# Middle four tiles of expert V rows: a spread activation matrix in DRAM and one pass over the V table

## Chip, core and metric

One core of a Trainium2 chip runs the whole program. The metric is the device time of one execution in microseconds. The profile names the engines PE (TensorE), DVE (VectorE), ACT (ScalarE), POOL (GpSimd) and SP (SyncE, which only issues transfers here); sixteen DMA engines move the data for all of them.

## Reference

One layer over 1024 tokens of width 1024, all in f32. First come two token mixers (a gated delta rule over four heads and a forgetting attention over eight), merged by two gates and put through a LayerNorm. Then comes PEER, the part that the change touches: each token picks 16 experts in each of 8 heads, 128 in all, out of 16384. Cut from the reference:

```python
def block(args):
    h_blk, e_blk, g_blk = args                     # 128 tokens, their 128 experts each, their gates
    u = jnp.take(u_tab, e_blk, axis=0)             # rows of 1024 floats
    act = jax.nn.gelu(jnp.einsum('td,tkd->tk', h_blk, u), approximate=False) * g_blk
    vv = jnp.take(v_tab, e_blk, axis=0)
    return jnp.einsum('tk,tkd->td', act, vv)
```

The result is added to 2**0.25 times the residual and put through a second LayerNorm. The U and the V table are 64 MB each (16384 rows of 4 KB).

## The kernel before

The tokens are cut into 8 tiles of 128 and 4 blocks (b = 0 to 3) of two tiles. `order()` writes out a list of 582 units (a step of the delta rule, an attention piece, a top-16 search and so on) that every engine walks in the same order; block b's mixers come first, then its choice of experts (`top`, `cand`, `sel`), which ends with the unit `idx`, where the chosen indices are transposed into `idxT`. The projections of block b + 1 are interleaved with the choice of block b; the last choice has none beside it.

The expert work runs alongside. After each unit every engine calls `experts(s)`, and the lists `DOTS` and `TOKS` that `pace()` plans say how much of it belongs to step s:

- A **U gather** (`gather_u`) is one indirect DMA from GpSimd: for one of the 128 choices of a tile, the 128 rows that its tokens chose, 128 x 4 KB, one row to a partition. VectorE multiplies it with the tile in `h_cur` and sums (one instruction, into a column of `dots`). When the 128 columns of a tile are there, ScalarE takes the gelu into `wgt`, VectorE multiplies with the gates, PE transposes, and ScalarE copies back into `dots`.
- A **V gather** (`gather_v`) is one indirect DMA too: the 128 rows that one token chose. Four such gathers make a quad. ScalarE spreads the weights into `wide32` (`spread`), and PE multiplies: for each of four tokens and two halves of 512 columns, one product with 32 columns of weights, which lands in the two PSUM banks `BY`. After the 32 quads of a tile VectorE adds the residual, takes the moments and normalises, and ScalarE stores the tile.

All gathers share `ring`, 18 places of 512 KB; from the place `WIDE` on, behind the last merge, 9 places in `arena` join it. `place_free` holds GpSimd until the reader of a place is done. At most `NU` = 16 U gathers and `NQ` = 8 quads are in flight. As planned by `pace()`, 768 U and 768 V gathers are done when the last `idx` ends; 256 of either kind remain for the tail. By stretches between the ends of `idx` (first half of block 0, second half, blocks 1, 2, 3, tail) the U counts are 106, 54, 188, 251, 169, 256 and the V counts 0, 64, 148, 248, 308, 256.

Of the kernel before, what the change touches and what calls it, by code (L numbers as in the profile page):

```python
# [10 lines left out]
D = 1024  # L11
# [20 lines left out]
NR = 18  # L32
NX = 9
NU, NQ = 16, 8
# [86 lines left out]

def pace():
# [3 lines left out]
    alone = UNITS.index(("top", NB - 1, 0))  # L126
    total = sum(share(kind, b) for kind, b, i in UNITS[first + 1:alone])
# [3 lines left out]
    dots, toks = [0], [0]  # L131
    ready, run, lately = 0, 0.0, 0
    for n, (kind, b, i) in enumerate(UNITS):
# [8 lines left out]
        else:  # L142

            run += share(kind, b) if n < alone else 0.0
# [5 lines left out]
    while dots[-1] < P * NT:  # L150
        dots.append(min(P * NT, dots[-1] + 4))
    dots += [P * NT] * 56
    opened = next(s for s in range(len(dots)) if dots[s] >= P) + 1
    for s in range(1, len(dots)):
        edge = P * (toks[-1] // P + 1)
        ready = dots[s] - P - LAG if dots[s] < P * NT else toks[-1] + 4
        step = 4
        if alone < s <= last + 1:

            begin = toks[alone]  # L160
            ready, step = begin + round((T * (NB - 1) - begin) * (s - alone) / (last + 1 - alone)), 8
# [7 lines left out]
    assert toks[-1] == P * NT and toks[-5] == P * NT  # L169
# [3 lines left out]
    for n in range(NT):  # L173
        for f in range(2, 32 // PHASE):
            assert phase_step(toks, n, f) < next(s for s in range(len(toks)) if toks[s] > P * n + 4 * PHASE * f)
    fetch = []
# [4 lines left out]
    for n in range(NT):  # L181
        assert begun[n] > dotted[n] and (n == 0 or begun[n] > summed[n - 1])
        assert n < 3 or fetch[n] >= summed[n - 3] + 2
        assert fetch[n] <= next(s for s in range(len(dots)) if dots[s] > P * n)

    place, upos, vpos = 0, [], []
    for s in range(1, len(dots)):
        du, dv = dots[s] - dots[s - 1], toks[s] - toks[s - 1]
# [8 lines left out]
    return dots, toks, dotted, begun, summed, fetch, upos, vpos  # L197

DOTS, TOKS, DOTTED, BEGUN, SUMMED, FETCH, UPOS, VPOS = pace()  # L200
# [4 lines left out]
def slots():  # L205

    begin = UNITS.index(("top", NB - 1, 0)) + 1
    at = UPOS + VPOS
    wide = min([UPOS[k] for k in range(DOTS[begin], P * NT)] + [VPOS[k] for k in range(TOKS[begin], P * NT)])
# [28 lines left out]
PLACED = UNITS.index(("idx", NB - 1, 0)) + 1  # L238
# [18 lines left out]
def item_loads():  # L257
# [8 lines left out]
    return value  # L266

LOADS = item_loads()
# [12 lines left out]
def transposed(n):  # L282

    return n // TT + 2 if n >= TT else n + 1

def build(nc, x, xT, w_qkv, w_z, w_sm, w_fqk, w_fv, w_mix, w_out, w_pq, conv_w, bias96, alog96,
          norm_w, ln, eu, ev, out):
    ctx = ExitStack()
    with ctx:  # L290
# [18 lines left out]
        d_h1 = dram("d_h1", SEQ, D)  # L309

# [15 lines left out]
        iota16 = sb("iota16", [P, TOPK])  # L326
# [7 lines left out]
        ring = sb("ring", [P, NR, D])  # L334
# [178 lines left out]
        s_yv, s_ys, s_y, s_out, s_h = sem("s_yv"), sem("s_ys"), sem("s_y"), sems("s_out", 3), sems("s_hc", 3)  # L513

# [5 lines left out]
        def place(p):  # L520

            if SLOT[p] < NR:
                return ring[:, SLOT[p], :]
            return arena[:, D * (SLOT[p] - NR + 1):D * (SLOT[p] - NR + 2)]

        hp = [banks[:, 1024 * (1 + k):1024 * (2 + k)] for k in range(2)]
        assert D * (NX + 1) <= after_rows and 32 % (2 * PHASE) == 0
# [13 lines left out]
        def _(sp):  # L541
# [210 lines left out]
        def _(pool):  # L752
# [7 lines left out]
            pool.iota(iota16[:, :], [[1, TOPK]], base=0, channel_multiplier=0, allow_small_or_imprecise_dtypes=True)  # L760
# [49 lines left out]
            def gather_v(k):  # L810
                n, i = divmod(k, P)
# [11 lines left out]
            for s in range(1, len(DOTS)):  # L823
                us, vs = range(DOTS[s - 1], DOTS[s]), range(TOKS[s - 1], TOKS[s])
# [1166 lines left out]
```

## Time and profile before

| | |
|---|---|
| Median of 3 runs | 3569.27 us (3568.06 to 3578.89) |
| Span of the profiled execution | 3575.8 us |
| Time of the profiled execution | not listed apart from its span; the span lies inside the range of the runs, 6.5 us above their median |
| Gathers (queue q0) | 1073.87 of 1290.18 MB moved |

The span runs from the first to the last instruction of the profiled execution.
### The profile page before, as it was taken

To read this page: it belongs to the slowest core of one execution; us is meant where nothing else is said; L and a number is where in the kernel's file an instruction comes from. 1 tells how busy PE (TensorE), PEld (TensorE's weight loads), DVE (VectorE), ACT (ScalarE), POOL (GpSimd) and SP (SyncE) were. 2 spreads that over 40 slices of the span, in tenths; PEclk is the share of its full clock that TensorE was granted. 3 is DMA by queue.
4 is the path that set the end of the run, shared out by engine and by line. 5 is a ranking of instruction groups with operands and counts; after the bars stand their busy time and mean duration, and the time that the engine had idled before them with its cause. 6 is when DMAs were issued, how large, how long until landed. Compare 5 with 4: busy or idle time off the path is not lost.

```text
span 3575.8 us, 37418 instructions
## 1 busy us (share of the span) xinstructions
PE 2446.3 (68%) x12224; PEld 1513.4 (42%) x12224; DVE 2097.0 (59%) x4939; ACT 655.0 (18%) x1652; POOL 2209.1 (62%) x2093
## 2 busy tenths in 40 slices
PE   8889993677976876667977877766797730133354
PEld 6676872444754544434735544433564310000000
DVE  5134899875477675554358776554447669744400
ACT  3331322332022213321003212321101000000000
POOL 1000577677547765677556766677767667777774
PEclk9899996888998987777988988867898865566588
DMA  5323999899989999999999999999999999999998
GB/s 171 91 87 136 363 401 360 336 392 402 409 312 373 400 412 360 350 381 384 415 402 351 408 405 394 369 377 371 398 413 410 409 410 409 410 409 409 409 410 324
DMA packets 367626, 1290.18 MB, mean 361 GB/s; under 512 B 39596, under 2 KB 68148, under 8 KB 362308
## 3 DMA queue, kind: packets, MB, share of 16 engines
q0 software_dynamic: 294912, 1073.87, 76.8%
q1 hardware_dynamic: 66760, 201.33, 15.2%
q10 hardware_dynamic: 5760, 12.59, 0.9%
q8 instruction: 98, 1.61, 0.2%
q14 instruction: 96, 0.79, 0.1%
HBM read 1274.65 MB, written 12.98 MB: 360 GB/s over the span
## 4 chain that ended last, share of the span: by engine, by line
PE 24%; DMA 22%; POOL 17%; DVE 16%; issue 15%; ACT 3%; DVEq 3%; ACTq 0%; POOLq 0%; SPq 0%
DMA ring<-in_ev,idxT 12%; PE banks L1570 10%; POOL ring L818 8%; DVE ring L1260 8%; POOL ring L804 8%; DMA ring<-in_eu,eidx 5%; PE banks L1580 4%; PE banks L1559 4%; DMA arena<-in_eu,eidx 3%; PE banks L1855 2%; PE banks L1702 1%; PE banks L1621 1%; DMA wslot<-in_w_mix 1%; POOL arena L818 1%; POOL arena L804 1%
## 5 line engine op out<-in xcount | busy, mean ns | idle before, releaser
L804 POOL DMA_INDIRECT ring<-in_eu,eidx x938 | 1044.4, 1113 | 875.5 <-DVE eidx L1529 393.4
L818 POOL DMA_INDIRECT ring<-in_ev,idxT x894 | 950.9, 1064 | 380.0 <-issue 245.7
L1559 PE MATMUL banks<-ring,wide 128*32 128x512 f32 x3576 | 631.5, 790 | 530.5 <-DMA ring<-in_ev,idxT 460.5
L1260 DVE CUSTOM_DVE_ANT_0 ring<-ring,h_cur 128x1024 f32<-128x1024 f32 x663 | 782.6, 1221 | 192.1 <-DMA ring<-in_eu,eidx 190.1
L1570 PE MATMUL banks<-arena,wslot 128*128 128x256 f32 (+2 forms) x3280 | 747.2, 386 | 21.9 <-DMA wslot<-in_w_pq 12.5
L1570 PEld LDWEIGHTS banks<-arena,wslot 128*128 128x128 f32 (+1 forms) x3280 | 622.4, 194 | 179.2 <-issue 70.9
L1559 PEld LDWEIGHTS banks<-ring,wide 128*32 128x32 f32 x3576 | 120.1, 130 | 851.7 <-DMA ring<-in_ev,idxT 431.5
L1260 DVE CUSTOM_DVE_ANT_0 ring<-ring,banks 128x1024 f32<-128x1024 f32 x275 | 329.3, 1217 | 110.8 <-DMA ring<-in_eu,eidx 106.8
L1580 PE MATMUL banks<-arena 128*128 128x128 f32 x1408 | 216.2, 312 | 42.3 <-ACT arena L995 26.1
L1580 PEld LDWEIGHTS banks<-arena 128*128 128x128 f32 x1408 | 202.9, 223 | 79.7 <-ACT arena L995 33.5
L1559 PE MATMUL banks<-arena,wide 128*32 128x512 f32 x520 | 138.6, 868 | 118.6 <-DMA ring<-in_ev,idxT 64.5
L1409 DVE TENSOR_REDUCE few<-banks 128x1 f32<-128x128 f32 (+3 forms) x64 | 48.4, 756 | 225.4 <-PE banks L1775 225.4
L1570 PE MATMUL banks<-ring,wslot 128*128 128x256 f32 (+1 forms) x656 | 151.4, 388 | 11.8 <-DMA wslot<-in_w_sm 7.4
L818 POOL DMA_INDIRECT arena<-in_ev,idxT x130 | 123.4, 949 | 40.3 <-issue 32.6
L1260 DVE CUSTOM_DVE_ANT_0 arena<-arena,banks 128x1024 f32<-128x1024 f32 x86 | 104.4, 1220 | 57.2 <-DMA arena<-in_eu,eidx 55.5
L1570 PEld LDWEIGHTS banks<-ring,wslot 128*128 128x128 f32 (+1 forms) x656 | 125.0, 193 | 30.1 <-issue 12.3
L1442 DVE TENSOR_TENSOR arena<-arena,banks 128x256 f32<-128x256 f32 x48 | 18.1, 418 | 195.2 <-PE banks L1570 195.2
L1550 PE MATMUL banks<-ident,wgt 128*128 128x128 f32 x8 | 2.7, 343 | 179.1 <-DVE wgt L1244 168.2
L1237 DVE SCALAR_TENSOR_TENSOR h_cur<-h_cur,banks 128x512 f32<-128x512 f32 x16 | 10.2, 680 | 188.6 <-PE banks L1559 188.6
L1559 PEld LDWEIGHTS banks<-arena,wide 128*32 128x32 f32 x520 | 24.4, 139 | 191.5 <-issue 78.2
L1575 PE MATMUL banks<-ident,arena 128*128 128x128 f32 x216 | 43.3, 348 | 83.2 <-DVE arena L1375 33.3
L1855 PE MATMUL banks<-wslot,arena 128*128 128x512 f32 x224 | 98.1, 595 | 2.9 <-issue 2.9
(302 smaller groups left out, 2810.9 us busy)
## 6 DMA issues: line engine op xcount, KB each, us to landing
wslot<-in_w_pq SPq DMA_DIRECT2D x64, 576.0 KB, 8.3
wslot<-in_w_mix SPq DMA_DIRECT2D x24, 1536.0 KB, 9.8
wslot<-in_w_qkv SPq DMA_DIRECT2D x48, 512.0 KB, 7.0
wslot<-in_w_fqk SPq DMA_DIRECT2D x32, 512.0 KB, 7.6
ring<-in_eu,eidx POOLq DMA_INDIRECT x938, 12.6
wslot<-in_w_out SPq DMA_DIRECT2D x7, 2048.0 KB, 10.4
ring<-in_ev,idxT POOLq DMA_INDIRECT x894, 12.4
wslot<-in_w_z SPq DMA_DIRECT2D x16, 512.0 KB, 6.7
```

Source lines behind the costliest of these rows:

```text
L804: pool.indirect_dma_start(out=place(UPOS[k]), out_offset=None, in_=eu, in_offset=bass.IndirectOffsetOnAxis(ap=eidx[:, n % (2 * TT), c // T ...
L818: pool.indirect_dma_start(out=place(VPOS[k]), out_offset=None, in_=ev, in_offset=bass.IndirectOffsetOnAxis(ap=idxT[:, n % (2 * TT), t:t + ...
L1260: dve.tensor_tensor_reduce(out=row, in0=row, in1=hp[0] if held else h_cur[:, n % 3, :] if n < NT - TT else hp[n % 2], scale=1.0, scalar=0. ...
L1409: dve.tensor_reduce(nm[:, r:r + 1], SB[b][r][:, 0:w], AX.X, ALU.max, negate=True).then_inc(s_sc[r], 1)
L1442: dve.tensor_tensor(mt[:, k, :], gates[:, k, :], B[3 * j + 1 - k][:, 0:T], ALU.mult)
L1559: last = pe.matmul(BY[k][32 * j:32 * j + 32, :], wide32[:, at:at + 32], place(VPOS[4 * q + j])[:, k * 512:(k + 1) * 512], start=(m == 0), ...
L1570: last = pe.matmul(bank, w[:, k0 + k, :], rhs[:, k, :], start=(k == 0), stop=(k == nk - 1))
L1575: last = pe.transpose(bank[:, h * P:(h + 1) * P], src[:, h, :], ident[:, :])
L1580: last = pe.matmul(bank[:, h * P:(h + 1) * P], lhs[:, h, :], rhs[:, h, :], start=start and (stop or h == 0), stop=stop and (start or h == ...
L1621: last = pe.matmul(PN[b][tt][:, :], xTs[b][:, k, tt * P:(tt + 1) * P], w[:, kk, :], start=(k == 0), stop=(k == KB - 1))
L1702: pe.matmul(B[4][:, :], ident[:, :], ident[:, None, :].to_broadcast([P, GH, P]), start=True, stop=False)
L1855: last = pe.matmul(WO[b][nh][tt][:, :], mixT[:, k, tt * P:(tt + 1) * P], w[:, k, :], start=(k == 0), stop=(k == KB - 1))
```

## The change

For tiles 2 to 5 (`DENSE`, tokens 256 to 767) no V row is gathered. Instead:

- **Spread.** For each of these tokens VectorE writes two 128x128 matrices, one comparing a row of 0 to 127 with the low 7 bits of each chosen expert, one comparing it with the high 7 bits and multiplied by the activation (`spots`). PE multiplies the two (one 128x128 product a token), which puts each activation at the place of its expert in a 128x128 grid, and ScalarE copies four such grids at a time from PSUM into `staged`. Each 16 tokens make 1 MB, which goes to the matrix `d_act` in DRAM (32 stores).
- **Product.** When all 512 tokens are spread and the last choice is done, SP reads the V table once, 128 pieces of 128 rows, into the eight slots of `wslot`, and `d_act` back in 16 pieces of 2 MB (runs of 512 bytes) into two places in `arena`. For each of the 128 pieces PE makes 8 products of 128 weight columns with 512 tokens, accumulated in the eight PSUM banks over all 128 pieces. ScalarE copies the eight banks out, PE transposes them, and VectorE and ScalarE finish tiles 2 to 5.
- **Order.** Tiles 6 and 7 keep their V gathers, which now begin behind the product, since that fills all banks. Their U gathers run beside it.
- **Room.** The ring has 13 places (five go to `staged` and to half of the comparison matrices), 12 U gathers and 5 quads may be in flight; seven places join at `WIDE`, which now lies at the start of the product. Tiles 6 and 7 take their dots from `h_cur` instead of a copy in PSUM.

As planned by the changed `pace()`, the U counts by the same stretches are 106, 54, 171, 229, 208, 256, the V gathers 0, 64, 128, 64, 0, 256, and the tokens spread 0, 0, 0, 184, 200, 128. Behind the last `idx` come the 128 remaining tokens with 80 U gathers; then `DENSE_AT`, and 176 U gathers beside the product.

```diff
-NR = 18
-NX = 9
-NU, NQ = 16, 8
+PLACES = 18
+NR = 13
+NX = 7
+DENSE = range(2, 6)
+ONE_BY_ONE = [n for n in range(NT) if n not in DENSE]
+HOT = range(P * DENSE[0], P * (DENSE[-1] + 1))
+STAGED = 16
+CHUNK = 8
+NCHUNK = P // CHUNK
+NV = 8
+NU, NQ = 12, 5
...
+        if HOT[0] <= toks[-1] <= HOT[-1]:
+            ready, step = edge - P + (dots[s] - edge) * P // (P - 24), 8
...
+        if toks[-1] > HOT[-1]:
+            if built is None:
+                built = s
+            step = 4
+            if dense[-1] < P or dense[max(0, s - 6)] < P:
+                ready = toks[-1]
+        dense.append(min(P, dense[-1] + 2) if built and s > built + 2 else 0)
         toks.append(max(toks[-1], min(ready // 4 * 4, edge, toks[-1] + step)))
...
+        d_act = dram("d_act", len(HOT) // STAGED, P, P * STAGED + 64)
...
+        staged = [ring[:, NR + 2 * k:NR + 2 * k + 2, :].rearrange("p a b -> p (a b)") for k in range(2)]
+        ones_at = [v.rearrange("p (t k c) -> p t k c", t=4, k=2) for v in (wide32[:, 0:D], ring[:, NR + 4, :])]
+        chunk = [arena[:, D + 4 * D * k:D + 4 * D * (k + 1)].rearrange("p (g c) -> p g c", g=len(HOT) // STAGED) for k in range(2)]
+        vtab = [wslot[:, k // 4, D * (k % 4):D * (k % 4 + 1)] for k in range(NV)]
+        yT = arena[:, D:5 * D].rearrange("p (k t) -> p k t", k=KB)
+        hy = arena[:, 9 * D:13 * D].rearrange("p (n c) -> p n c", n=len(DENSE))
+        SUM = [BY, B[0:2], B[2:4], B[4:6]]
...
+            sp.wait_ge(s_ixT, transposed(NT - 1))
+            for i in range(P):
+                c = i // CHUNK
+                if i % CHUNK == 0:
+                    if c == 0:
+                        for k in range(2):
+                            sp.wait_ge(s_stored[k], 16 * (len(HOT) // STAGED // 2))
+                    if c >= 2:
+                        sp.wait_ge(s_spot, len(HOT) // 4 + CHUNK * (c - 1))
+                    sp.dma_start(chunk[c % 2], d_act[:, :, c * CHUNK * STAGED:(c + 1) * CHUNK * STAGED].rearrange("g j x -> j g x")
+                                 ).then_inc(s_chunk[c % 2], 16)
+                if i >= NV:
+                    sp.wait_ge(s_spot, len(HOT) // 4 + i - NV + 1)
+                sp.dma_start(vtab[i % NV], ev[i * P:(i + 1) * P, :]).then_inc(s_w[i % NV // 4][i % 4], 16)
...
                 if p == WIDE:
-                    pool.wait_ge(s_hTe, TT * NB)
-                    pool.wait_ge(s_h1st, 16 * NB)
+                    for k in range(2):
+                        pool.wait_ge(s_stored[k], 16 * (len(HOT) // STAGED // 2))
+                    pool.wait_ge(s_spot, len(HOT) // 4)
+                    pool.wait_ge(s_ixT, transposed(NT - 1))
...
+                for k in range(hot(TOKS[s - 2]) // STAGED, hot(TOKS[s - 1]) // STAGED):
+                    act.wait_ge(s_sev, STAGED // 4 * (k + 1))
+                    act.dma_start(d_act[k, :, 0:P * STAGED], staged[k % 2]).then_inc(s_stored[k % 2], 16)
+                for q in range(hot(TOKS[s - 1]) // 4, hot(TOKS[s]) // 4):
+                    k, m = divmod(q, STAGED // 4)
+                    act.wait_ge(s_spot, q + 1)
+                    if m == 0 and k >= 2:
+                        act.wait_ge(s_stored[k % 2], 16 * (k // 2))
+                    act.activation(staged[k % 2].rearrange("p (i t) -> p t i", t=STAGED)[:, 4 * m:4 * m + 4, :],
+                                   BY[q % 2][:, :].rearrange("p (t i) -> p t i", t=4), ACT.Copy).then_inc(s_sev, 1)
+                if s == SUMMED[DENSE[0]]:
+                    act.wait_ge(s_spot, len(HOT) // 4 + P)
+                    for k in range(KB):
+                        act.activation(yT[:, k, :], B[k][:, :], ACT.Copy).then_inc(s_sev, 1)
...
+            def spots(q):
+
+                n, m = DENSE[q // 32], q % 32
+                cols, rows_ = expert_rows(n)
+                if m == 0:
+                    dve.wait_ge(s_ixT, transposed(n))
+                    dve.wait_ge(s_wm, n + 1)
+                    dve.drain()
+                    dve.tensor_scalar(rows_.bitcast(U32), cols, 7, None, ALU.logical_shift_right)
+                    dve.tensor_scalar(cols, cols, P - 1, None, ALU.bitwise_and)
+                    dve.drain()
+                    dve.tensor_copy(rows_, rows_.bitcast(U32))
+                    dve.tensor_copy(cols.bitcast(F32), cols)
+                    dve.drain()
+                    dve.wait_ge(s_w32, columns(n) + 1)
+                if q >= 2:
+                    dve.wait_ge(s_spot, q - 1)
+                if q == 0:
+                    dve.wait_ge(s_vq, T // 4)
+                for r in range(4):
+                    t = 4 * m + r
+                    dve.tensor_scalar(ones_at[q % 2][:, r, 0, :], iota[:, :], cols.bitcast(F32)[:, t:t + 1], None, ALU.is_equal)
+                    last = dve.tensor_scalar(ones_at[q % 2][:, r, 1, :], iota[:, :], rows_[:, t:t + 1], dots[:, n % 2, t:t + 1],
+                                             ALU.is_equal, ALU.mult)
+                last.then_inc(s_hot, 1)
...
                         pe.wait_ge(s_wm, n + 1)
-                        pe.wait_ge(s_yev, n)
+                        if n <= DENSE[0]:
+                            pe.wait_ge(s_yev, n)
+                        elif n in DENSE:
+                            pe.wait_ge(s_sev, 32 * (n - DENSE[0]))
+                        else:
+                            pe.wait_ge(s_yev, DENSE[0] + 1 if n - 1 in DENSE else n)
                         pe.transpose(BY[0][:, 0:P], wgt[:, :], ident[:, :]).then_inc(s_wT, 1)
...
+                    pe.wait_ge(s_hot, q + 1)
+                    if q >= 2:
+                        pe.wait_ge(s_sev, q - 1)
+                    for r in range(4):
+                        last = pe.matmul(BY[q % 2][:, r * P:(r + 1) * P], ones_at[q % 2][:, r, 0, :], ones_at[q % 2][:, r, 1, :],
+                                         start=True, stop=True)
+                    last.then_inc(s_spot, 1)
+                for i in range(DONE[s - 1], DONE[s]):
+                    c, ii = divmod(i, CHUNK)
+                    if i == 0:
+                        pe.wait_ge(s_sev, len(HOT) // 4)
+                        pe.wait_ge(s_ixT, transposed(NT - 1))
+                    if ii == 0:
+                        pe.wait_ge(s_chunk[c % 2], 16 * (c // 2 + 1))
+                    pe.wait_ge(s_w[i % NV // 4][i % 4], 16 * (LAST_LOAD.get((i % NV // 4, i % 4), 0) + i // NV + 1))
+                    acts = chunk[c % 2][:, :, STAGED * ii:STAGED * (ii + 1)]
+                    for k in range(KB):
+                        last = pe.matmul(B[k][:, :], vtab[i % NV][:, k * P:(k + 1) * P], acts, start=(i == 0), stop=(i == P - 1))
+                    last.then_inc(s_spot, 1)
+                if s == SUMMED[DENSE[0]]:
+                    pe.wait_ge(s_sev, len(HOT) // 4 + KB)
+                    for k in range(len(DENSE)):
+                        for half in range(2):
+                            last = transpose4(SUM[k][half], yT[:, 4 * half:4 * half + 4, k * P:(k + 1) * P])
+                        last.then_inc(s_spot, 1)
+                for q in range(alone(TOKS[s - 1]) // 4, alone(TOKS[s]) // 4):
```

## Rows read from the trace of the kernel before

**Rows 1.** The page: span, busy time of PE, gather queue, bytes

```profile
span 3575.8 us, 37418 instructions
...
PE 2446.3 (68%) x12224; PEld 1513.4 (42%) x12224; DVE 2097.0 (59%) x4939; ACT 655.0 (18%) x1652; POOL 2209.1 (62%) x2093
...
q0 software_dynamic: 294912, 1073.87, 76.8%
...
HBM read 1274.65 MB, written 12.98 MB: 360 GB/s over the span
```

**Rows 2.** Tile idxT: ScalarE's copies of the transposed choices, first and last start

```profile
L1174 ACT ACTIVATE idxT<-banks x3: 384/384/385, 1349.7 to 2900.8; 128x256 uint32<-128x256 f32 x3
L1169 ACT ACTIVATE idxT<-banks x2: 277/278/278, 573.9 to 765.6; 128x128 uint32<-128x128 f32 x2
```

**Rows 3.** Timeline of ScalarE, window 2126:2200: the copy behind block 2's choice

```profile
2172.23 0.38 ACT L1174 ACTIVATE idxT<-banks 128x256 uint32<-128x256 f32 x1
```

**Rows 4.** Windows between those choices: busy of five engines, PE clock, DMA share, GB/s

```profile
574.00:766.00 192.00, 115.68 (x706) 74.83 (x710) 172.54 (x488) 60.89 (x150) 134.00 (x124) 0.78 0.93 348
766.00:1350.00 584.00, 458.47 (x2121) 297.17 (x2113) 382.73 (x984) 112.00 (x298) 380.45 (x332) 0.88 0.99 385
1350.00:2172.00 822.00, 628.45 (x3126) 395.35 (x3126) 495.72 (x1175) 174.99 (x437) 560.91 (x503) 0.85 1.00 385
2172.00:2901.00 729.00, 547.09 (x2934) 312.25 (x2932) 396.14 (x994) 134.30 (x320) 514.34 (x483) 0.85 1.01 393
2901.00:3576.00 675.00, 200.93 (x1042) 37.11 (x1042) 328.78 (x541) 11.29 (x31) 465.68 (x496) 0.65 1.00 398
```

**Rows 5.** PE's waits in windows 766:1350, 1350:2172, 2172:2901: total us, times, longest

```profile
PE banks L1559 <- DMA ring<-in_ev,idxT: 85.5, 20, 13.1
...
PE banks L1559 <- DMA ring<-in_ev,idxT: 127.6, 34, 10.5
...
PE banks L1559 <- DMA ring<-in_ev,idxT: 113.8, 35, 7.2
```

**Rows 6.** Window 2705:2901, between the last merge and the last choice, columns as Rows 4

```profile
2705.00:2901.00 196.00, 145.97 (x855) 72.94 (x851) 121.37 (x524) 20.00 (x69) 139.81 (x144) 0.87 1.03 409
```

**Rows 7.** The page's costliest group on DVE: the U dots

```profile
L1260 DVE CUSTOM_DVE_ANT_0 ring<-ring,h_cur 128x1024 f32<-128x1024 f32 x663 | 782.6, 1221 | 192.1 <-DMA ring<-in_eu,eidx 190.1
```

**Rows 8.** The page's DMA issues: U gathers, median us to landing

```profile
ring<-in_eu,eidx POOLq DMA_INDIRECT x938, 12.6
```

**Rows 9.** Timeline of VectorE, window 1360:1368: four 128x128 TENSOR_SCALAR

```profile
1359.69 0.98 DVE L1347 TENSOR_SCALAR arena<-arena 128x128 f32<-128x128 f32 x4
```

**Rows 10.** Lines of PE by form: 128x128 products, and transposes

```profile
L1580 PE MATMUL banks<-arena 128*128 128x128 f32 x1408 | 216.2, 312 | 42.3 <-ACT arena L995 26.1 <-DVE arena L1388 9.4 <-ACT arena L992 4.1
...
L1575 PE MATMUL banks<-ident,arena 128*128 128x128 f32 x216 | 43.3, 348 | 83.2 <-DVE arena L1375 33.3 <-DVE arena L1355 22.1 <-DVE arena L1402 12.3
```

**Rows 11.** Lines of ScalarE by form: a PSUM bank of 128x512 copied

```profile
L1114 ACT ACTIVATE arena<-banks 128x512 f32<-128x512 f32 x31 | 18.5, 597 | 282.3 <-PE banks L1570 282.3
```

**Rows 12.** Timeline of PE, window 2660:2700: 128- and 32-column weights

```profile
2665.61 1.92 PE L1559 MATMUL banks<-ring,wide 128*32 128x512 f32 x16 [0.54 <-DMA ring<-in_ev,idxT]
2667.47 14.00 PE L1855 MATMUL banks<-wslot,arena 128*128 128x512 f32 x32
...
2690.49 3.64 PE L1559 MATMUL banks<-ring,wide 128*32 128x512 f32 x16 [6.14 <-DMA ring<-in_ev,idxT]
```

**Rows 13.** A window of unbroken PE work, columns as Rows 4

```profile
2590.00:2645.00 55.00, 55.00 (x280) 43.31 (x273) 22.82 (x44) 3.58 (x10) 34.08 (x31) 1.00 1.02 416
```

**Rows 14.** DMA issues: 2 MB load, 1 MB store, 512-byte pieces

```profile
wslot<-in_w_out SPq DMA_DIRECT2D x7, 2048.0 KB, 10.4
...
d_h<-arena SPq DMA_DIRECT2D x4, 1024.0 KB, 10.2
...
arena<-d_fv SPq DMA_DIRECT2D x4, 512.0 KB, 18.3
```

**Rows 15.** The chain that ended last, its last long piece

```profile
3537.50 26.86 DMA ring<-in_ev,idxT
```

More of the change, by code:

```diff
@@ L125, in pace @@
     last = UNITS.index(("idx", NB - 1, 0))
-    alone = UNITS.index(("top", NB - 1, 0))
-    total = sum(share(kind, b) for kind, b, i in UNITS[first + 1:alone])
+    total = sum(share(kind, b) for kind, b, i in UNITS[first + 1:last])
     second = UNITS.index(("att", 1, 0))
     levels = sum(share(kind, b) for kind, b, i in UNITS[first + 1:second])
-    dots, toks = [0], [0]
+    dots, toks, dense = [0], [0], [0]
     ready, run, lately = 0, 0.0, 0
@@ L142, in pace @@
         else:
-            run += share(kind, b) if n < alone else 0.0
+            run += share(kind, b) if n < last else 0.0
             if n < second:
@@ L149, in pace @@
         dots.append(max(dots[-1], min(want, ready, dots[-1] + 8)))
-    while dots[-1] < P * NT:
-        dots.append(min(P * NT, dots[-1] + 4))
-    dots += [P * NT] * 56
     opened = next(s for s in range(len(dots)) if dots[s] >= P) + 1
-    for s in range(1, len(dots)):
-        edge = P * (toks[-1] // P + 1)
[L156 to L161, printed above, removed]
+    built = None
+    s = 0
+    while len(dots) < len(UNITS) + 2 or toks[-1] < P * NT:
+        s += 1
+        if s == len(dots):
+            dots.append(min(P * NT, dots[-1] + 4))
+        edge = P * (toks[-1] // P + 1)
+        ready, step = dots[s] - P - LAG, 4
+        if HOT[0] <= toks[-1] <= HOT[-1]:
+            ready, step = edge - P + (dots[s] - edge) * P // (P - 24), 8
+        if s > last + 1:
+            ready, step = toks[-1] + 8, 8
         if s <= second:
@@ L167, in pace @@
             ready = toks[-1]
+        if toks[-1] > HOT[-1]:
[5 more added lines that the diff above has]
+        dense.append(min(P, dense[-1] + 2) if built and s > built + 2 else 0)
         toks.append(max(toks[-1], min(ready // 4 * 4, edge, toks[-1] + step)))
-    assert toks[-1] == P * NT and toks[-5] == P * NT
+    for _ in range(6):
+        dots.append(dots[-1])
+        toks.append(toks[-1])
+        dense.append(dense[-1])
     dotted = [next(s for s in range(len(dots)) if dots[s] >= P * (n + 1)) for n in range(NT)]
@@ L172, in pace @@
     summed = [next(s for s in range(len(toks)) if toks[s] >= P * (n + 1)) for n in range(NT)]
-    for n in range(NT):
+    for n in ONE_BY_ONE:
         for f in range(2, 32 // PHASE):
             assert phase_step(toks, n, f) < next(s for s in range(len(toks)) if toks[s] > P * n + 4 * PHASE * f)
+    for n in range(NT):
+        assert begun[n] > dotted[n] and (n == 0 or begun[n] > summed[n - 1])
+    for n in DENSE:
+        assert summed[n] < next(s for s in range(len(dots)) if dots[s] > P * (n + 2))
+        summed[n] = dense.index(P) + 1 + n - DENSE[0]
+    assert begun[DENSE[-1] + 1] - 1 > summed[DENSE[0]]
+    assert toks[UNITS.index(("sel", NB - 1, 0))] >= P * NT - 2 * T
     fetch = []
@@ L181, in pace @@
     for n in range(NT):
-        assert begun[n] > dotted[n] and (n == 0 or begun[n] > summed[n - 1])
-        assert n < 3 or fetch[n] >= summed[n - 3] + 2
+        if n in (3, 4):
+            assert fetch[n] >= summed[n - 3] + 2
+        elif n > 4:
+            assert fetch[n] >= dotted[n - 3]
         assert fetch[n] <= next(s for s in range(len(dots)) if dots[s] > P * n)
+    gelu = [max(dotted[n], begun[n - 1] if n else 0) for n in range(NT)]
     place, upos, vpos = 0, [], []
     for s in range(1, len(dots)):
-        du, dv = dots[s] - dots[s - 1], toks[s] - toks[s - 1]
+        du, dv = dots[s] - dots[s - 1], alone(toks[s]) - alone(toks[s - 1])
         assert du + dv <= NR
@@ L265, in item_loads @@
             value[b, name, n] = count[half, q]
-    return value
-LOADS = item_loads()
+    return value, count
+LOADS, LAST_LOAD = item_loads()
 def chosen(b, i):
@@ L284, in transposed, with columns @@
     return n // TT + 2 if n >= TT else n + 1
+def columns(n):
+    return sum(1 if k in DENSE else 32 // PHASE for k in range(n))
 def build(nc, x, xT, w_qkv, w_z, w_sm, w_fqk, w_fv, w_mix, w_out, w_pq, conv_w, bias96, alog96,
```

109 lines of the change are left out of this document (68 added, 41 removed).

## Prediction

> **What bounds the kernel now.** I read the page first: of 1290 MB, 1074 go through the queue of the gathers [rows 1]. Then I looked for the ends of the choices, where the plan's stretches end: 574, 766, 1350, 2172 and 2901 us [rows 2, 3]. In the windows between them the DMA share is 0.93 in the first and 0.99 to 1.01 in the four others [rows 4]. So from 574 us on the transfers set the pace. A gather is 1073.87 / 2048 = 0.524 MB, which is 1.28 us at 409 GB/s [rows 1, 6]; the tail's 512 gathers make 656 of its 675 us [rows 4]. PE waits for V rows for 85.5, 127.6 and 113.8 us in blocks 1 to 3 [rows 5], which is little: PE is itself busy for 458 of 584, 628 of 822 and 547 of 729 us [rows 4]. In the tail it is busy for 201 of 675 at a granted clock of 0.65. The reader should see two kernels here: up to 2901 us the engines have nearly as much to do as the DMA, behind it only the DMA does.
>
> **What the change takes and adds in bytes.** 512 V gathers go: 268 MB. The V table is 67 MB, the matrix 34 MB written and 34 MB read. The balance is 134 MB less, 328 us at 409 GB/s. That would be the gain if the transfers stayed the bound everywhere. The rest of this part asks where they don't.
>
> **Up to the last choice.** Up to 766 us the plan is unchanged: 766.
>
> Block 1 has 20 of 148 V and 17 of 188 U gathers fewer. PE's waits shrink by 20/148 of 85.5, 12 us; the dots save 17 x 1.18 = 20 us of VectorE (782.6 us for 663 [rows 7]), of which I count 17: 584 - 29 = 555. Ends: 584 if nothing follows, 537 by bytes (37 x 1.28). The smaller ring (12 U in flight instead of 16) costs nothing as long as 12 x 1.28 = 15 us covers the 12.6 us to landing [rows 8]; if it doesn't, the gain of 29 is lost.
>
> Block 2 has 184 of 248 V gathers fewer: 184/248 of 127.6 us is 95, so 822 - 95 = 727. Block 3 loses all V waits, 114 us, and gets 39 U gathers more, 46 us on VectorE. I count these as exposed, because 54 of its U gathers now lie in the last choice, where there were none and VectorE was busy for 121 of 196 us with other work [rows 6]: 729 - 114 + 46 = 661.
>
> Spreading costs VectorE two 128x128 instructions a token; four such took 0.98 us [rows 9], so 0.49 us a token, 90 us in block 2 and 98 in block 3. PE's part is two records of 216.2/1408 = 0.154 us [rows 10], 0.31 us a token, less than the V products that it replaces (sixteen records in 1.92 to 3.64 us for four tokens [rows 12]). ScalarE copies a bank in 0.60 us [rows 11] for four tokens. I cost all this at nothing here, since VectorE idles for 326 of 822 and 333 of 729 us [rows 4], part of it behind PE's waits for V rows, which go. If that cover is gone, it costs 188 us. The lower ends are VectorE's own work with everything else hidden: 496 - 22 x 1.18 + 90 = 560 in block 2, and 396 + 46 + 98 = 540 in block 3; the upper ends are the lengths now, 822 and 729. The waits that come in matter more than the work: VectorE may be only two quads ahead of PE, and PE two ahead of ScalarE, and behind each stand that engine's next unit and its dots.
>
> Behind the last choice, VectorE has 80 dots and 128 tokens: 94 + 63 = 157, taken as 160; the 80 gathers need 102 us beside it. If the handshakes add up (0.60 + 8 x 0.154 us for 32 quads), 58 more. Then the last store must land and the first 2 MB piece come back: 10.2 and 10.4 us for 1 and 2 MB [rows 14], taken as 25. A 512 KB load in runs of 512 bytes took 18.3 us [rows 14], so 2 MB of them bound the piece at 73. SP, which issues the loads, has nothing else left by then. GpSimd waits at `WIDE` for the same stores, and behind that wait stand the 176 U gathers, for which the 896 us below leave time enough. Of the 32 stores the 24 before the last choice lie on ScalarE's queue behind its own copies; a buffer is wanted again after 16 tokens, some 50 us in blocks 2 and 3, and a 1 MB store landed in 10.2 us, so they cost nothing; if they landed five times later, ScalarE's units would wait behind the next copy.
>
> **The product.** The nearest row is the output projection: 128x128 weights, 512 columns, f32, 32 records in 14.00 us [rows 12], 0.4375 us a record at a granted clock of 1.00, which unbroken PE work had for 55 us with the DMA full beside it [rows 13]. A product is two records, so a piece of the table takes 16 records, 7.0 us, and 128 pieces 896 us. The ends are 1.92 us for 16 records with 32 weight columns, four column groups of which run side by side [rows 12], and 14.0 at half the clock; I take 7.0, since form, type and clock are the same. The Trainium skill ("TensorE: Matmul & The Clock Gate", section "Back-to-back issue gap") gives about 131 ns as the sustained spacing of 512-column matmuls with their weight loads, and "FP8 and Floating Point Precision" (section "TensorE Precision Notes") counts four passes for true FP32: 0.52 us a product, 537 us in all by these pages as an estimate, and a sum of 3785 instead of 4144. The rows have 0.875 us a product, so here the trace does not agree.
>
> What can hide under these 896 us is small. Each piece needs 0.79 MB, 112 GB/s; with the 176 U gathers it is 193 MB, 472 us of transfers. The DMA, which is full now, is idle for almost half of the product, and the 256 V gathers of tiles 6 and 7 cannot use this time, since they wait for the banks (20 of them may be in flight). This is where the 328 us go.
>
> **Behind it.** Eight copies of 0.60 us [rows 11] and 32 transposes of two records at 43.3/216 = 0.20 us [rows 10] are 18 us. Three of the four finished tiles stand ahead of tile 6's weights on ScalarE. One finish with its store takes 3575.8 - 3537.50 - 26.86 = 11.4 us at the kernel's end [rows 1, 15], so these cost between 0 and 34; I take 20, and 40 in all. Then 236 V gathers, 302 us, and 12 for the last finish.
>
> **Sum:** 766 + 555 + 727 + 661 + 160 + 25 + 896 + 40 + 302 + 12 = 4144, against a span of 3575.8; the median of the runs is 6.5 below that span, so I give 4140. Ahead of the last choice 192 us are won; behind it 1435 us stand where 675 were.
>
> **Rivals.**
> *The bytes decide* (the faster side). If the product ran as fast as its transfers and the blocks followed their bytes, the time would be 3576 - 328 = 3248. For it speaks the DMA share of 1.00. It decides as long as the product exceeds its 472 us of transfers by less than 328: under 6.25 us a piece. The rows have 7.0, and VectorE's 560 and 540 us forbid that blocks 2 and 3 follow their bytes. Chance 0.03, two thirds of it faster, the rest near no change.
> *The products stand closer than rows 12.* Down to the transfers' 472 us, this gives 4144 - 424 = 3720. The 32-column records speak for it, the 128-column ones against it: 0.03. The figure of the Trainium skill above ("TensorE: Matmul & The Clock Gate", section "Back-to-back issue gap") is of this kind.
> *Blocks at VectorE's floor.* 537, 560 and 540: 4144 - 18 - 167 - 121 = 3838. For it speaks that transfers were the only bound; against it, that the units are chains over several engines. 0.09 for the times up to 3950.
> *Handshakes eat the gain.* Blocks as long as now: 4144 + 29 + 95 + 68 = 4336; with the 188 us of spreading exposed, 4524. 0.18.
> *The product starves.* Pieces of the matrix that take 73 us where eight table pieces take 56 add 15 x 17 = 255, which is 4399; if PE also loses its clock in half of the pieces, 448 more. 0.05: 112 GB/s is far below what the DMA moves now.
> *My sum,* 3950 to 4300: 0.62.
>
> **The numbers.** The range 3870 to 4400 leaves out the first two rivals (0.06), a third of the floor case (0.03), a third of the handshakes (0.06) and the starving (0.05): 0.20. A change of 0.3%, 11 us, is about what this measurement can tell from none. Faster has 0.02, no change 0.01, slower 0.97.
>
> **What would show it.** In the trace after, PE busy without a break for some 900 us near the end at a clock of 1.00, 16 records in 7.0 us; a DMA share near 1 in the first part of that stretch and near a quarter behind the U gathers; the last idxT copy near 2709 us; a last stretch of V gathers of about 300 us at 409 GB/s. I am wrong if a piece takes clearly less than 7 us, or if blocks 2 and 3 come out under 600 us or longer than now.

## The result, and the profile after

The changed kernel takes 4494.2 us (median of 4 runs, 4483.3 to 4500.6) beside 3571.7 for the kernel before: a ratio of 1.257, 95% interval 1.254 to 1.260. It is slower, as forecast, and 94 us beyond the upper end of the range.

The page of the profiled execution (span, busy engines, DMA share in 40 slices, gather queue, two groups):

```profile
span 4488.4 us, 40366 instructions
...
PE 3319.7 (74%) x13280; PEld 2117.1 (47%) x13280; DVE 2326.1 (52%) x5980; ACT 780.7 (17%) x1749; POOL 1698.5 (38%) x1581
...
DMA  4237999999999954567666544559999533431998
...
q0 software_dynamic: 221184, 805.40, 48.2%
...
L1705 PE MATMUL banks<-arena,wslot 128*128 128x512 f32 x2048 | 889.9, 597 | 93.5 <-DMA wslot<-in_ev 93.5
...
L1692 PE MATMUL banks<-wide 128*128 128x128 f32 x512 | 120.3, 409 | 319.8 <-DVE wide L1391 319.8
```

Beside [rows 1], 268 MB of gathers are gone and PE is busy for 873 us more. The DMA line shows what the prediction did not have: digits of 4 to 7 from the 15th slice to the 27th. In blocks 2 and 3, long ahead of the product, the DMA engines are thus idle for 0.28 and 0.44 of the time (shares of 0.72 and 0.56 in the windows below). The ends of the choices, as in [rows 2, 3], blocks 0, 1 and 3 first, then block 2:

```profile
L1271 ACT ACTIVATE idxT<-banks x3: 366/384/412, 1315.9 to 3014.3; 128x256 uint32<-128x256 f32 x3
L1264 ACT ACTIVATE idxT<-banks x2: 277/286/294, 578.1 to 772.2; 128x128 uint32<-128x128 f32 x2
```

```profile
2182.32 0.41 ACT L1271 ACTIVATE idxT<-banks 128x256 uint32<-128x256 f32 x1
```

Windows between them, then to the start and the end of the product and to the end (columns as in [rows 4]):

```profile
772.00:1316.00 544.00, 445.76 (x2041) 293.08 (x2041) 360.29 (x944) 110.59 (x299) 333.27 (x297) 0.89 0.98 377
1316.00:2182.00 866.00, 605.04 (x2742) 455.95 (x2742) 551.27 (x1506) 220.12 (x470) 315.79 (x299) 0.81 0.72 259
2182.00:3014.00 832.00, 511.19 (x2115) 405.57 (x2115) 516.31 (x1450) 179.77 (x344) 222.79 (x208) 0.71 0.56 190
3014.00:3217.00 203.00, 62.28 (x257) 56.86 (x257) 191.16 (x488) 35.09 (x35) 136.93 (x107) 0.56 0.93 334
3217.00:4138.00 921.00, 889.38 (x2048) 392.59 (x2048) 179.05 (x291) 0.31 (x1) 184.03 (x160) 0.98 0.57 199
4138.00:4488.00 350.00, 187.62 (x1060) 40.11 (x1058) 33.43 (x55) 13.04 (x36) 222.00 (x236) 0.73 0.91 363
```

Term by term, predicted and measured: up to the second choice 766 and 772; block 1 555 and 544; block 2 727 and 866; block 3 661 and 832; to the start of the product 185 and 203; the product 896 and 921; behind it 354 and 350. Blocks 2 and 3 make 310 of the 344 us by which the span of 4488 exceeds the sum of 4144, and they are not shorter than before but longer (822 and 729). In block 3 the DMA share is 0.56, VectorE is busy for 516 of 832 us and PE for 511, at a clock of 0.71: nothing is full. What PE waits for, and what VectorE waits for, in block 3 (us in total, times, longest). PE has two rows because the two pairs of comparison matrices lie in `wide32` and in the ring; in block 2 they are 108.7 and 82.6:

```profile
PE banks L1692 <- DVE wide L1391: 133.5, 20, 14.0
PE banks L1692 <- DVE ring L1391: 80.3, 18, 9.2
```

```profile
DVE arena L1573 <- PE banks L1732: 111.8, 8, 14.4
DVE few L1540 <- PE banks L1937: 91.3, 16, 8.3
```

A step of the last merge, PE first and then VectorE (start, us, engine, line; in brackets the idle time before it and who ended it):

```profile
2559.65 7.95 PE L1732 MATMUL banks<-arena,wslot 128*128 128x256 f32 x36
2574.37 2.07 PE L1692 MATMUL banks<-wide 128*128 128x128 f32 x8 [6.77 <-DVE wide L1391]
2576.23 12.42 PE L1732 MATMUL banks<-arena,wslot 128*128 128x256 f32 x48
2596.46 2.08 PE L1692 MATMUL banks<-ring 128*128 128x128 f32 x8 [7.81 <-DVE ring L1391]
```

```profile
2567.71 0.75 DVE L1573 TENSOR_TENSOR arena<-arena,banks 128x256 f32<-128x256 f32 x2 [14.27 <-PE banks L1732]
...
2568.88 1.22 DVE L1360 CUSTOM_DVE_ANT_0 ring<-ring,h_cur 128x1024 f32<-128x1024 f32 x1
...
2572.31 0.09 DVE L1360 DVE_READ_ACCUMULATOR2_ANT dots<- 128x1 f32 x1
2572.31 0.31 DVE L1390 TENSOR_SCALAR wide<-iota,idxT 128x128 f32<-128x128 f32 x1
...
2573.98 0.34 DVE L1391 TENSOR_SCALAR wide<-iota,gate,dots 128x128 f32<-128x128 f32 x1
2588.76 0.75 DVE L1573 TENSOR_TENSOR arena<-arena,banks 128x256 f32<-128x256 f32 x2 [14.45 <-PE banks L1732]
```

The two take turns. VectorE gets the merge's product (L1573) at 2567.71, does three dots and then the spread (L1390, L1391) until 2574.3. PE has finished its unit at 2567.6 and stands at the spread's product (L1692) until 2574.37, with the next unit, 12.42 us of the merge's products (L1732), behind it. VectorE, done, waits 14.45 us for that unit. A step takes 21 us.

### The profile page after: what moved, and what is told of

Read it like the earlier page. It is cut to its first block, busy times and chain, and to the rows that moved or that the text cites. A ratio compares the mean times of both kernels' runs of the same rounds, so it can differ in the third digit from the quotient of the medians.

```text
span 4488.4 us, 40366 instructions
## 1 busy us (share of the span) xinstructions
PE 3319.7 (74%) x13280; PEld 2117.1 (47%) x13280; DVE 2326.1 (52%) x5980; ACT 780.7 (17%) x1749; POOL 1698.5 (38%) x1581
## 4 chain that ended last, share of the span: by engine, by line
PE 47%; DVE 27%; issue 7%; DMA 6%; POOL 6%; DVEq 3%; ACT 3%; another core or an unknown queue 2%; ACTq 0%; POOLq 0%; SPq 0%
PE banks L1705 20%; DVE ring L1360 12%; PE banks L1732 11%; POOL ring L890 4%; DMA ring<-in_ev,idxT 4%; PE banks L1742 3%; PE banks L1692 3%; PE banks L2017 3%; PE banks L1934 2%; PE banks L1721 2%; POOL ring L876 2%; PE banks L1957 1%; DMA ring<-in_eu,eidx 1%; DVE wide L1391 1%
## 5 line engine op out<-in xcount | busy, mean ns | idle before, releaser
L876 POOL DMA_INDIRECT ring<-in_eu,eidx x1006 | 1151.9, 1145 | 1830.3 <-DVE dots L1360 1163.9
L1360 DVE CUSTOM_DVE_ANT_0 ring<-ring,h_cur 128x1024 f32<-128x1024 f32 x898 | 1062.6, 1220 | 126.9 <-DMA ring<-in_eu,eidx 126.1
L1705 PE MATMUL banks<-arena,wslot 128*128 128x512 f32 x2048 | 889.9, 597 | 93.5 <-DMA wslot<-in_ev 93.5
L890 POOL DMA_INDIRECT ring<-in_ev,idxT x486 | 489.4, 1007 | 909.5 <-PE banks L1721 704.6
L1732 PE MATMUL banks<-arena,wslot 128*128 128x256 f32 (+2 forms) x3280 | 774.1, 396 | 21.4 <-DMA wslot<-in_w_pq 8.1
L1732 PEld LDWEIGHTS banks<-arena,wslot 128*128 128x128 f32 (+1 forms) x3280 | 646.9, 201 | 145.6 <-issue 30.7
L1705 PEld LDWEIGHTS banks<-arena,wslot 128*128 128x128 f32 x2048 | 392.6, 192 | 590.4 <-issue 590.4
L1721 PE MATMUL banks<-ring,wide 128*32 128x512 f32 x1944 | 342.3, 801 | 250.0 <-DMA ring<-in_ev,idxT 234.3
L1692 PE MATMUL banks<-wide 128*128 128x128 f32 x512 | 120.3, 409 | 319.8 <-DVE wide L1391 319.8
L1692 PEld LDWEIGHTS banks<-wide 128*128 128x128 f32 x512 | 103.6, 300 | 338.8 <-DVE wide L1391 338.3
L936 ACT ACTIVATE ring<-banks 128x512 f32<-128x512 f32 x128 | 134.1, 1048 | 648.4 <-PE banks L1692 648.4
L1692 PE MATMUL banks<-ring 128*128 128x128 f32 x512 | 116.6, 400 | 162.9 <-DVE ring L1391 162.9
L1692 PEld LDWEIGHTS banks<-ring 128*128 128x128 f32 x512 | 101.7, 295 | 176.7 <-DVE ring L1391 175.2
L1573 DVE TENSOR_TENSOR arena<-arena,banks 128x256 f32<-128x256 f32 x48 | 18.1, 419 | 282.8 <-PE banks L1732 282.8
L1732 PE MATMUL banks<-ring,wslot 128*128 128x256 f32 (+1 forms) x656 | 151.3, 387 | 11.2 <-DMA wslot<-in_w_sm 6.8
```

The lines of the kernel that those rows point to most:

```text
L876: pool.indirect_dma_start(out=place(UPOS[k]), out_offset=None, in_=eu, in_offset=bass.IndirectOffsetOnAxis(ap=eidx[:, n % (2 * TT), c // T ...
L890: pool.indirect_dma_start(out=place(VPOS[k]), out_offset=None, in_=ev, in_offset=bass.IndirectOffsetOnAxis(ap=idxT[:, n % (2 * TT), t:t + ...
L936: act.activation(staged[k % 2].rearrange("p (i t) -> p t i", t=STAGED)[:, 4 * m:4 * m + 4, :], BY[q % 2][:, :].rearrange("p (t i) -> p t i ...
L1360: dve.tensor_tensor_reduce(out=row, in0=row, in1=hp if held else h_cur[:, n % 3, :], scale=1.0, scalar=0.0, op0=ALU.mult, op1=ALU.add, acc ...
L1692: last = pe.matmul(BY[q % 2][:, r * P:(r + 1) * P], ones_at[q % 2][:, r, 0, :], ones_at[q % 2][:, r, 1, :], start=True, stop=True)
L1705: last = pe.matmul(B[k][:, :], vtab[i % NV][:, k * P:(k + 1) * P], acts, start=(i == 0), stop=(i == P - 1))
```

## The experiments

Three theories of where the 344 us went were put to the runs. Theory 1: the turn-taking just seen, PE standing at the spread of its own step with VectorE's next unit behind it. Theory 2: VectorE's added work itself. Theory 3: PE's lower granted clock, 0.71 in block 3, as a cause and not as a consequence of its standing. Beside them, it was open whether the product's price is PE's own or that of its loads.

**PE and VectorE wait for nothing of each other in the spread.** Kernel `e1_free`, in which PE multiplies a constant matrix in place of the spread's:

```diff
-                    dve.wait_ge(s_spot, q - 1)
+                    dve.wait_ge(s_hot, q - 1)
...
-                    pe.wait_ge(s_hot, q + 1)
+                    if q % 32 == 0:
+                        pe.wait_ge(s_w32, columns(DENSE[q // 32]) + 1)
...
-                        last = pe.matmul(BY[q % 2][:, r * P:(r + 1) * P], ones_at[q % 2][:, r, 0, :], ones_at[q % 2][:, r, 1, :],
+                        last = pe.matmul(BY[q % 2][:, r * P:(r + 1) * P], ident[:, :], ident[:, :],
```

> All work of the changed kernel stays, but PE multiplies a constant 128x128 matrix with itself and waits for nothing of VectorE's spread, and VectorE waits for nothing of PE; the activations therefore do not reach the product. Theory 1 (PE stands at the spread of the same step, with its next unit behind it, and VectorE then stands at that unit): the 191 and 214 us that PE waits in blocks 2 and 3 go, the blocks fall from 866 and 832 to about 700 and 660 us, the time to about 4160. Theory 2 (VectorE's added work is what lengthens the blocks): blocks stay within 30 us, the time above 4430. Theory 3 (the lower clock of PE in these blocks, 0.81 and 0.71, is the cause and not a consequence): PE still works at under 0.8 in block 3, time above 4400.

4086.8 us, ratio 1.144 (1.142 to 1.146). Its blocks 2 and 3:

```profile
1315.00:2041.00 726.00, 574.52 (x2741) 438.96 (x2742) 543.31 (x1487) 218.87 (x470) 311.86 (x295) 0.84 0.85 308
2041.00:2699.00 658.00, 435.20 (x2117) 352.46 (x2116) 522.24 (x1469) 177.71 (x345) 231.46 (x211) 0.78 0.70 239
```

726 and 658 us with VectorE as busy as in the changed kernel (543 and 522 us): 140 and 174 us went with the two waits alone, and the blocks are close to the terms of the prediction, 727 and 661. Theory 2 is out, since the work is all there, and so is theory 3 as the first cause, since the clock rose to 0.84 and 0.78 once the waits were gone. The clock is part of the price, though: nearly the same number of records kept PE busy for 605 and 511 us in the changed kernel and for 575 and 435 here, so up to 30 and 76 of the 140 and 174 us are due to the lower clock that went with the standing. The remaining 92 of the 407 us belong to the experiment: the product begins 111 us behind the last choice instead of 203, as it no longer waits for VectorE's last spread.

**Seven eighths of VectorE's spread left out, the waits kept.** Kernel `e2_little`:

```diff
-                for r in range(4):
+                for r in range(4 if q < 2 else 1):
                     t = 4 * m + r
-                    dve.tensor_scalar(ones_at[q % 2][:, r, 0, :], iota[:, :], cols.bitcast(F32)[:, t:t + 1], None, ALU.is_equal)
+                    if q < 2:
+                        dve.tensor_scalar(ones_at[q % 2][:, r, 0, :], iota[:, :], cols.bitcast(F32)[:, t:t + 1], None, ALU.is_equal)
                     last = dve.tensor_scalar(...)
```

> Seven of the eight VectorE instructions of each four spread tokens are left out (the first eight tokens keep them), all waits stay; the matrix is therefore wrong. Theory 1: PE still stands behind the dots of each step; of 4.2 us of wait a quad about 2 go, the blocks fall by about 190 us together, the tail by 60, time about 4240. Theory 2: all of VectorE's spread, 249 us in the blocks and 85 behind them, less an eighth, comes off: about 4200, and PE's waits for VectorE vanish.

4320.8 us, ratio 1.210 (1.207 to 1.212). Most of the work is gone, and in block 3 PE still waits:

```profile
PE banks L1693 <- DVE wide L1392: 104.7, 20, 12.1
...
PE banks L1693 <- DVE ring L1392: 52.8, 13, 7.6
```

157 us of 214 remain, with the dots of the step still ahead of the signal (the next run moves them). Both theories had expected more of this run than the 173 us it gave. The choices end at 1317.5, 2123.1 and 2881.9, so blocks 2 and 3 are 806 and 759 us long with an eighth of the spread's work, longer than 726 and 658 with all of it and no waits: in these runs the work costs by what it adds to the wait.

**Spread ahead of the dots.** Kernel `e3_spots_first` moves one loop of VectorE:

```diff
+                for q in range(hot(TOKS[s - 1]) // 4, hot(TOKS[s]) // 4):
+                    spots(q)
                 for k in range(DOTS[s - 1], DOTS[s]):
...
-                for q in range(hot(TOKS[s - 1]) // 4, hot(TOKS[s]) // 4):
-                    spots(q)
```

> VectorE spreads ahead of the step's dots instead of behind them; the work is the same. Theory 1: PE waits shorter by the two to four dots of a step (1.15 us each), about 250 instead of 405 us in the two blocks, time about 4340. Theory 2: the same VectorE work, no change, 4494.

4336.5 us, ratio 1.215 (1.213 to 1.217), as theory 1 had it. No work changed. In block 3:

```profile
PE banks L1692 <- DVE wide L1391: 95.6, 18, 15.1
...
PE banks L1692 <- DVE ring L1391: 37.8, 16, 6.9
```

133 us instead of 214, in block 2 127 instead of 191.

**PE and ScalarE one step behind.** Kernel `e4_lag1`, with ScalarE's stores, its copies and PE's spread products in this order:

```diff
-                for k in range(hot(TOKS[s - 2]) // STAGED, hot(TOKS[s - 1]) // STAGED):
+                for k in range(hot(TOKS[s - 3]) // STAGED, hot(TOKS[s - 2]) // STAGED):
...
-                for q in range(hot(TOKS[s - 1]) // 4, hot(TOKS[s]) // 4):
+                for q in range(hot(TOKS[s - 2]) // 4, hot(TOKS[s - 1]) // 4):
...
-                for q in range(hot(TOKS[s - 1]) // 4, hot(TOKS[s]) // 4):
+                for q in range(hot(TOKS[s - 2]) // 4, hot(TOKS[s - 1]) // 4):
```

> PE's spread products, ScalarE's copies and the stores come one step later in their engines' order than VectorE's spread. Theory 1: PE does its next unit while VectorE has its dots and the spread, the waits of 405 us shrink to under 100, blocks about 710 and 680, time about 4190. Theory 2: no change, 4494. Theory 3: no change in the blocks as long as the clock stays low.

4188.9 us, ratio 1.172 (1.170 to 1.174): 305 us for three shifted indices. Blocks 2 and 3, and PE's waits in block 3:

```profile
1323.00:2037.00 714.00, 556.17 (x2736) 425.13 (x2734) 543.80 (x1489) 218.44 (x470) 310.37 (x295) 0.88 0.86 314
2037.00:2727.00 690.00, 464.58 (x2124) 374.36 (x2123) 522.14 (x1468) 181.45 (x345) 226.18 (x211) 0.74 0.67 228
```

```profile
PE banks L1692 <- DVE ring L1391: 66.0, 11, 11.7
...
PE banks L1692 <- DVE wide L1391: 30.0, 8, 7.2
```

The blocks are 714 and 690 us, and the time is as expected; the waits are not. 96 us of them remain in block 3 and 84 in block 2, 180 where under 100 were expected for both together.

**Two steps behind, three pairs of matrices.** Kernel `e7_lag2`:

```diff
-NR = 13
-NX = 7
+NR = 12
+NX = 8
...
-        ones_at = [... (wide32[:, 0:D], ring[:, NR + 4, :])]
+        ones_at = [... (wide32[:, 0:D], ring[:, NR + 4, :], ring[:, NR + 5, :])]
...
-                if q >= 2:
-                    dve.wait_ge(s_spot, q - 1)
+                if q >= 3:
+                    dve.wait_ge(s_spot, q - 2)
```

with the indices of the kernel above shifted by one more step and the matrices taken by `q % 3`.

> PE and ScalarE two steps behind VectorE, with three pairs of comparison matrices instead of two and a ring of 12 places. Theory 1: the 85 and 96 us that PE still waits in blocks 2 and 3 with one step mostly go, the time comes near the version without waits, about 4100. Rival: the rest of the wait is VectorE's own rate (it is busy for 550 of 721 us), then no gain, 4180.

4193.9 us, ratio 1.173 (1.171 to 1.176): no gain over one step. PE's waits for the spread fell from 84 and 96 us to 61 and 74, and the time did not follow: block 3 was about 30 us shorter, block 2 was 13 longer. Whether the smaller ring took back a gain was not separated.

**One product of eight.** Kernel `e5_one_of_eight`, made from `e4_lag1`:

```diff
-                    for k in range(KB):
+                    for k in range(KB if i in (0, P - 1) else 1):
                         last = pe.matmul(B[k][:, :], vtab[i % NV][:, k * P:(k + 1) * P], acts, start=(i == 0), stop=(i == P - 1))
```

> As the version with PE one step behind (4189 us), but of the eight products of each table piece seven are left out (the first and the last piece keep all), so the sums lack most of their columns; all loads stay. If PE's 16 records of 7.0 us bound the product, its 920 us fall to what the transfers need, about 480 us, and the time to about 3750. Rival: loads bound it (PE shows 90 us of waits for them), then it stays above 4050.

3757.0 us, ratio 1.051 (1.047 to 1.055). The product's stretch:

```profile
2906.00:3395.00 489.00, 195.26 (x284) 65.26 (x284) 178.99 (x291) 0.31 (x1) 182.57 (x158) 0.62 1.03 375
```

489 us at a DMA share of 1.03, against the 472 of its bytes; 432 of 921 us were PE's own. The rival is out.

**Both costs gone.** Kernel `e8_free_one` has the edits of `e1_free` and `e5_one_of_eight`.

> As the version in which PE waits for nothing of the spread (4087 us), with seven of eight products left out as well. If the two costs add up, 4087 - 440 = 3650: with neither the waits nor the product the time would still be above the kernel before, since the blocks no longer follow their bytes. Rival (the bytes decide once both are gone): near 3250 to 3400.

3714.0 us, ratio 1.039 (1.036 to 1.042), 64 us above what was expected. The product's stretch:

```profile
2808.00:3362.00 554.00, 198.34 (x284) 62.89 (x284) 259.98 (x466) 0.31 (x1) 251.81 (x210) 0.62 1.03 378
```

It has 65 us more than in the kernel above, since VectorE's last dots and U gathers that lay ahead of the product now lie in it (260 us of VectorE instead of 179). The time is still above the kernel before, with 134 MB less to move: the bytes do not decide even here.

**The meeting alone, in the kernel before.** Kernel `e9_meet`:

```diff
                     last.then_inc(s_vq, 1)
+                if UNITS.index(("idx", 1, 0)) + 1 < s <= UNITS.index(("idx", NB - 1, 0)) and DOTS[s] > DOTS[s - 1]:
+                    pe.wait_ge(s_dot, DOTS[s])
```

> The kernel before, with one wait alone added: between the second and the last choice PE waits at the end of each step until VectorE has done that step's dots. No work is added. Theory 1 says that such a meeting in the same step costs by itself: PE's next unit stands behind 2 to 4 dots of 1.15 us in some 140 steps, so blocks 2 and 3 grow by 100 to 250 us, the time to 3670 to 3820. Rival: in a kernel whose blocks follow the transfers the meeting hides behind them, under 3600.

3691.0 us, ratio 1.032 (1.030 to 1.034). Blocks 2 and 3, PE's three largest waits for dots in them, and VectorE's largest wait for PE:

```profile
1352.00:2237.00 885.00, 652.75 (x3126) 414.00 (x3126) 496.30 (x1176) 175.49 (x439) 556.83 (x503) 0.83 0.94 357
2237.00:3023.00 786.00, 571.35 (x2932) 331.39 (x2932) 396.09 (x994) 133.87 (x318) 512.83 (x484) 0.82 0.95 364
```

```profile
PE banks L1572 <- DVE dots L1260: 89.9, 23, 13.0
PE banks L1797 <- DVE dots L1260: 38.9, 17, 5.7
PE banks L1857 <- DVE dots L1260: 35.2, 8, 7.3
```

```profile
DVE arena L1442 <- PE banks L1572: 204.2, 16, 13.7
```

The same wait of VectorE in blocks 2 and 3 of the kernel before:

```profile
DVE arena L1442 <- PE banks L1570: 131.7, 16, 13.9
```

No instruction was added but a wait, and 117 us came: the two blocks are 885 and 786 us long instead of 822 and 729 [rows 4], and the DMA share in them fell from 1.00 and 1.01 to 0.94 and 0.95. VectorE waits 72 us longer for PE in the merge once PE waits for VectorE: the same turn-taking, in a kernel that has nothing of the change.

**The smaller ring alone.** Three kernels, made from the kernel before: `e6_ring13` has all of this, `e10_places` all but the line of `NU` and `NQ`, `e11_flight` that line alone.

```diff
-NR = 18
+PLACES = 18
+NR = 13
...
-NU, NQ = 16, 8
+NU, NQ = 12, 5
...
-        ring = sb("ring", [P, NR, D])
+        ring = sb("ring", [P, PLACES, D])
```

> The kernel before with one part of the change alone: a ring of 13 places, 12 U gathers and 5 quads in flight instead of 18, 16 and 8. If 12 gathers in flight cover the landing time as the prediction has it, 3572 within 0.5%. Rival: the smaller store of gathered rows lets every hold-up of an engine reach the DMA, then blocks 1 to 3 lose several per cent, 3630 to 3700.

> The kernel before with 13 ring places and the old 16 U gathers and 8 quads in flight. If the places are what cost 2.1% (rows wait in them until an engine's order comes to them), 3650; if it is the number in flight, 3575.

> The kernel before with 18 ring places, but 12 U gathers and 5 quads in flight. If the places are what cost 2.1%, 3575; if it is the number in flight, 3650.

3652.8 us, ratio 1.021 (1.019 to 1.024), with both; 3643.9, 1.020 (1.018 to 1.022), with 13 places; 3576.5, 1.001 (0.9995 to 1.002), with fewer in flight. It is the places. With 13 places the last choice ends 66 us later than in [rows 2], and the tail is as long as before:

```profile
L1175 ACT ACTIVATE idxT<-banks x3: 361/383/384, 1373.5 to 2967.0; 128x256 uint32<-128x256 f32 x3
```

## Why the prediction was right and wrong

**Slower: right, and for the reason given.** The product is the largest cost. A record took 889.9/2048 = 0.4345 us (predicted 0.4375, [rows 12]) and the stretch 921 us instead of 896, 31 of it waits while U gathers ran beside it. The two parts of the stretch, with the U gathers and behind them:

```profile
3217.00:3520.00 303.00, 271.38 (x608) 119.02 (x609) 179.05 (x291) 0.31 (x1) 184.03 (x160) 0.95 1.03 393
3520.00:4138.00 618.00, 618.00 (x1442) 273.56 (x1440) 0.00 (x0) 0.00 (x0) 0.00 (x0) 1.00 0.35 105
```

PE is busy without a break for 618 us at a clock of 1.00 while the DMA moves 105 GB/s: this is the idle DMA that was forecast (share 0.35 where I had about a quarter). The Trainium skill ("TensorE: Matmul & The Clock Gate", section "Back-to-back issue gap") gives about 131 ns for a matmul of 512 columns in a sustained stream; these rows, at 0.4345 us a record, do not show it for this f32 product. What stands behind the product (350 against 354) and block 1 (544 against 555) came close to what was worked out; block 1 did so with the smaller ring put at nothing, of which below.

**The step that failed** is "I cost all this at nothing here, since VectorE idles for 326 of 822 and 333 of 729 us". The spread's work was indeed covered: `e1_free` has all of it and blocks near the predicted ones. What was not covered is the wait between VectorE and PE. The prediction says "The waits that come in matter more than the work", but its sum has no term for them, and they are priced only as a rival (0.18). They made blocks 2 and 3 139 and 171 us longer than their terms, and longer than now, which the prediction had given as a sign of being wrong. Much of the idle time that I counted as cover was not free: VectorE spent it waiting for PE's next unit, and the change put that unit behind a signal that VectorE gives last in the step. Its two largest waits in block 3 of the kernel before:

```profile
DVE few L1409 <- PE banks L1775: 83.1, 15, 9.5
DVE arena L1442 <- PE banks L1570: 61.6, 8, 9.4
```

PE's waits of 191 and 214 us replaced its waits for V rows, which were 128 and 114 us [rows 5] but were met by transfers under way, not by an engine that in turn waits for PE. The rival's range, 4336 to 4524, holds the result, but not by what it counts: its lower end takes the blocks as long as now, and they were 44 and 103 us longer; its upper end adds the spread's 188 us of work, which `e1_free` has without that cost. That `e1_free` comes within 4 us of both terms is in part luck, since the terms leave out the smaller ring.

**Prices that did not decide.** VectorE's part of the spread cost what was forecast: in the step shown above the eight instructions of four tokens run from 2572.31 to 2574.32, 0.50 us a token against 0.49. ScalarE's copy of a bank, which now writes with a step of 16 elements, took 1.04 instead of 0.60 us:

```profile
L936 ACT ACTIVATE ring<-banks x128: 1024/1042/1096, 1530.9 to 3155.1; 128x512 f32<-128x512 f32 x128
```

The 18 us more ahead of the product are two errors that nearly cancel, which is luck. PE's last spread product and its first of the table:

```profile
3153.04 2.04 PE L1692 MATMUL banks<-ring 128*128 128x128 f32 x8
3217.78 2.90 PE L1705 MATMUL banks<-arena,wslot 128*128 128x512 f32 x3 [62.70 <-DMA wslot<-in_ev]
```

The last spread was done 141 us behind the last choice, where 160 were taken; then PE waited 63 us for the last store and the first loads, beside U gathers, where 25 were taken.

**The ring** was costed at nothing by the wrong quantity. Landing time against gathers in flight holds (`e11_flight`), but a place is held until the in-order reader comes to it, and five places fewer cost 2.0% of the kernel before, 23 us of it in block 1 (607 us between its choices in `e10_places`, 584 before). How much of that the changed kernel pays was not separated: its block 1, the stretch in which it would show by itself, was 11 us shorter than predicted. The gains of `e1_free`, `e3_spots_first` and `e4_lag1` are not the ring's, since these have the 13 places too.

**Not settled:** which part of the remaining 84 and 96 us of waits in `e4_lag1` is VectorE's own rate, and what sets the 726 and 658 us of `e1_free`, where neither VectorE (543 and 522 us) nor PE nor the DMA (0.85 and 0.70) is full. And no version run here beats the kernel before: with the wait shifted away 4189 us remain, and even without seven eighths of the product 3757.

## What to carry to other kernels

Idle time of an engine is cover only if the new work meets nobody there: before costing a handshake at nothing, write down for one step what stands behind each of the two waits in its queue, and if each is the other's next unit, let the reader run a step behind. In this kernel a transfer that feeds a queue has been under way for a while when the wait is reached; an engine's result of the same step has not. And a plan that saves bytes is worth its bytes only in stretches that stay bound by them: here 0.79 MB take 1.9 us to move at 409 GB/s and took 7.0 us to multiply.

## What the runs showed of the hardware

Copying four 128x128 grids from PSUM to a layout with a step of 16 elements took ScalarE 1.04 us, against 0.60 us for the same 128x512 elements written in a row. In the step shown, a record of VectorE's comparing instruction lasted 0.31 us with one scalar by pointer and 0.34 with two and a multiplication, but eight such records in a row took 2.01 us together: they overlap, and a sum of their lengths overstates the price. Loads in runs of 512 bytes beside whole rows held the DMA engines busy for 0.35 at 105 GB/s, where the gathers of whole rows give 1.03 at 409 GB/s [rows 6]; by these figures a byte of the mixture cost about a third more of their time, as an estimate. Whether the short runs alone make the difference was not separated.
